# Start addresses of the matmul operands moved to multiples of 64 bytes, and 64 key tiles done in products of 256 columns

## The chip, the cores and the metric

The kernel runs on one core of one Trainium2 chip. The metric is the device time of one execution in microseconds (us); lower is better. Engines are named as the profile names them: PE is the matrix engine (PEld its weight loads), DVE the vector engine, ACT the scalar engine, POOL the GpSimd engine, SP the engine whose queue issues most transfers.

## What is computed

One decoder block on 256 tokens of width 1024, in float32. A mixer (convolution and dilated attention, gated, with one output projection) is added to x; then a retrieval layer is added:

```
def peer(xn, w_q, sub_keys, u_tab, v_tab):
    q = (xc @ w_q).reshape(TOKEN_CHUNK, PEER_HEADS, 2, half)
    s = einsum('thpd,hpnd->thpn', q, sub_keys)
    top_s, top_i = top_k(s, 16); ... best_s, best_c = top_k(cand, 16)
    e = i1 * PEER_N_KEYS + i2                      # expert of 16384
    gate = softmax(best_s)
    h = einsum('thkd,td->thk', u_tab[e], xc)
    act = gelu(h) * gate
    return einsum('thk,thkd->td', act, v_tab[e])
```

The kernel does not gather experts. It multiplies the tokens with all 16384 rows of u_tab and all 16384 rows of v_tab, and masks by a gate matrix.

## The kernel before

All data pass through 128 partitions. Weights come as 332 tiles of 128 partitions by 1024 float32 values (512 KB): 76 front tiles (projections of the mixer and the queries), 128 tiles of u_tab (the key tiles), 128 tiles of v_tab (the value tiles). Each tile goes through a ring of four slots in three buffers. SP loads it into `raw`; ACT rounds it to `hi` (`split_hi`, L335); POOL or DVE writes the remainder `raw - hi` to `lo` (`split_lo`, L354). Tokens and activations are split in the same way, so a float32 product is the sum of three products in the type float32r: hi with hi, hi with lo, lo with hi. `by_dve` (L337) says who makes which remainder: POOL alone in the first 64 key tiles, POOL and DVE by turns in the last 64 and in the last 64 value tiles, DVE alone in the first 64 value tiles.

The stages, in order of time:

- the front, 0 to some 255 us. `product` (L1236) does a slice of 128 weights by 256 tokens in three matmuls of 256 columns, with one weight load for each matmul. A tile is eight slices, 24 matmuls. The tokens are read from `nrm` (a view of `norm_space`) or from `rounded` (a view of `rounded_space`). L1266 and L1273 do the same in two loops for the first three tiles, L1343 with tokens as the weights for six tiles.
- the first 64 key tiles, some 259 to 435 us: `u_tile` (L1483), the same 24 matmuls, banks 4 and 5 by turns. ACT reads the bank through Gelu into `act` (`gelu`, L642). Beside it DVE selects the experts.
- the last 64 key tiles, some 435 to 632 us: `wide_tile` (L1489). Since `nrm` holds hi and lo of a slice side by side, the two products of `hi` are one matmul of 512 columns (L1499), and `lo` with the hi tokens one of 256 (L1501): 16 matmuls for a tile. The bank then holds two halves that must be added. ACT copies one half to `half_sum` (`copy_cross`, L666), DVE adds the other (`add_halves`, L1167), ACT applies Gelu to the sum (`gelu_sum`, L671). Beside it, every four tiles, DVE makes one-hot matrices for 16 tokens and PE multiplies them to gates (`gates`, L1513, 32 short matmuls of 64 columns in float16), and DVE multiplies the gates into `act` (L1154).
- the value tiles, some 632 to 1004 us: `v_tile` (L1554). The weights of PE are here activations (`act_hi`, `act_lo`, a second view of `norm_space`, filled by ACT at L677 and DVE at L1161), and `hi` or `lo` of the value tile is what streams, in 12 matmuls of 512 columns a tile (L1564; the last two tiles at L1590). In the first 64 tiles the gates of the other half of `act` are made as before.

Each engine's program is written out by hand with semaphores; nothing is reordered by a planner. PE waits for the remainder of its tile (`wait_lo`), and before it reuses bank 4 or 5 for what reads that bank.

Buffers lie one behind the other in the order of the code. The constant `SHIFT = 8` puts `nrm` 32 bytes behind the start of `norm_space`, and `rounded` 128 bytes behind that of `rounded_space`:

```
norm_space = sb("norm_space", [P, KB * 2 * T + SHIFT], F32R)
nrm = norm_space[:, SHIFT:].rearrange("p (k a t) -> p k a t", a=2, t=T)
picked_acts = norm_space[:, 0:RING * 2 * T].rearrange(...)
```

Of the kernel before, what the change touches and what calls it, by code (L numbers as in the profile page):

```python
# [15 lines left out]
P = 128  # L16
D = 1024
# [29 lines left out]
SHIFT = 8  # L47
# [117 lines left out]
def hybrid_block(nc, x_t, front, cols, rel_bias, onehot, sub_keys, u_tiles, v_tiles, out):  # L165
    bias_row = nc.dram_tensor("bias_row", (HEADS, BW), F32, kind="Internal").ap()
    toeplitz = nc.dram_tensor("toeplitz", (HEADS, P * BW), F32, kind="Internal").ap()
    with ExitStack() as ctx:
        def sb(name, shape, dt=F32, stack=ctx):
            return stack.enter_context(nc.sbuf_tensor(name, shape, dt))  # L170

        def sem(name):
            return ctx.enter_context(nc.semaphore(name))
# [7 lines left out]
        picked_acts = norm_space[:, 0:RING * 2 * T].rearrange("p (k a t) -> p k a t", a=2, t=T)  # L181
# [45 lines left out]
        half_sum = sb("half_sum", [P, 2, T])  # L227
        ohB = sb("ohB", [P, 2, TOK // PAIR, 2, HALF, PAIR], F16)
        raw = sb("raw", [P, RING, D])
        hi = sb("hi", [P, RING, D], F32R)  # L230
        lo = sb("lo", [P, RING, D], F32R)
# [61 lines left out]
        crossed, added, gelu_done = sem("crossed"), sem("added"), sem("gelu_done")  # L293
# [35 lines left out]
        def split_hi(act_e, base, it, j):  # L329

            s = slot_of(base, j)
            wait_raw(act_e, base, it, j)
            if not (isinstance(it, int) and base + 4 * it + j < RING):
                wait(act_e, pe_step, step_of(base - 4, it, j))
            act_e.copy(hi[:, s, :], raw[:, s, :]).then_inc(hi_ready, 1)  # L335
# [129 lines left out]
        def _(a):  # L465
# [196 lines left out]
            def copy_cross(it, j):  # L662

                a.wait_ge(pe_step, it * 4 + (S_U + HALF + j + 1))
                a.wait_ge(gelu_done, it * 4 + (HALF + j - 1))
                a.copy(half_sum[:, j % 2, :], bank[4 + j % 2][:, T:2 * T]).then_inc(crossed, 1)  # L666

            def gelu_sum(base, it, j):

                a.wait_ge(added, it * 4 + (base + j + 1))  # L670
                a.activation(act[:, it * 4 + (HALF + base + j), :], half_sum[:, (base + j) % 2, :], ACT.Gelu)\  # L671
                 .then_inc(gelu_done, 1)

# [5 lines left out]
            def key_round(it, first=False, last=False):  # L679
                for j in range(RING):  # L680
                    if last and j == RING - 1:
                        a.wait_ge(gated, GROUPS_N)
                        a.wait_ge(blocks_free, 1)
                        for first_act in range(AHEAD):
                            a_split(first_act, 0, 0)
                    copy_cross(it, j)
                    if not (first and j == 0):
                        gelu_sum(-1, it, j)
                    split_hi(a, U0 + HALF + LEAD, it, j)

            key_round(0, first=True)
            with a.Fori(1, HALF // RING - 1) as it:
                key_round(it)
            key_round(HALF // RING - 1, last=True)
            gelu_sum(HALF - 1, 0, 0)
# [22 lines left out]
        def _(dve):  # L718
# [445 lines left out]
            def add_halves(it, j):  # L1164

                dve.wait_ge(crossed, it * 4 + (j + 1))
                dve.tensor_tensor(half_sum[:, j % 2, :], bank[4 + j % 2][:, 0:T], half_sum[:, j % 2, :], ALU.add)\  # L1167
                   .then_inc(added, 1)

            def gate_body(half, it, first=False, last=False):  # L1170

                base = U0 + HALF if half == 0 else V0
                for j in range(RING):
# [16 lines left out]
                    if half == 0:  # L1190
                        if last and j == RING - 1:
                            for first_act in range(AHEAD):
                                low_part(first_act, 0, 0)
                        add_halves(it, j)
# [27 lines left out]
        def _(pe):  # L1222
# [260 lines left out]
            def u_tile(base_i, it, j):  # L1483

                wait(pe, gelu_done, it * 4 + (base_i + j - 1))
                ins = product(bank[4 + j % 2][:, 0:T], j, [(k, k) for k in range(KB)], nrm_hi, nrm_lo, U0 + base_i, it, j)
                ins.then_inc(pe_step, 1)

            def wide_tile(it, j, last=False):  # L1489

                b = bank[4 + j % 2]
                if isinstance(it, int) and it == 0 and j < 2:
                    pe.wait_ge(gelu_done, HALF + j - 1)
                else:
                    pe.wait_ge(added, it * 4 + (j - 1))
                wait_lo(pe, U0 + HALF, it, j)
                for k in range(KB):
                    unit = slice(k * P, (k + 1) * P)
                    pe.matmul(b[:, :], hi[:, j, unit], nrm[:, k, :, :].rearrange("p a t -> p (a t)"),  # L1499
                              start=k == 0, stop=False, skip_group_check=True)  # L1500
                    ins = pe.matmul(b[:, 0:T], lo[:, j, unit], nrm_hi[:, k, :],  # L1501
                                    start=False, stop=k == KB - 1, skip_group_check=True)
                    if last and k == RING - 1:
                        ins.then_inc(blocks_free, 1)
                ins.then_inc(pe_step, 1)
# [37 lines left out]
            def u_and_gates(it, last=False):  # L1543
                for j in range(RING):
                    for g in groups_ahead(it, j):
                        gates(0, it, g)
                    wide_tile(it, j, last and j == RING - 1)
# [117 lines left out]
```

## Time and profile before

| | |
|---|---|
| median of 2 runs | 1012.49 us (1012.19 to 1012.79) |
| profiled execution, its own time | 1012.39 us |
| span of the profile, first to last instruction | 1010.6 us |
| busy, share of the span | PE 100%, PEld 89%, DVE 79%, ACT 52%, POOL 46% |
| mean granted TensorE clock | 1.000 of full speed |

The span is the time between the first and the last instruction of the trace; the 1.8 us between it and the run's time lie outside the instructions. In the timeline, a row's first number is the start in us, the second how long it and what is merged with it took, and the count at the end how many instructions are merged. Matmuls overlap: one of 256 columns shows 0.28 us, but the next starts 0.11 us later. So the price of a matmul in a stream is read from start to start, not from its duration.

### The profile page before, as it was taken

The page shows a single profiled execution, that of the slowest core. Times are in us where ns is not written, and L with a number is a line of the kernel's source. Part 1 is how long each engine was busy: PE and PEld are TensorE (multiplying, and loading weights), DVE is VectorE, ACT ScalarE, POOL GpSimd, SP SyncE. Part 2 cuts the span into 40 slices and gives each one's busy share as a digit, 9 for nine tenths or more (in the row PEclk, how much of TensorE's full clock was granted, in tenths as well). Part 3 has the DMA queues.
Part 4 walks back from the last instruction along what each step waited for, and adds up shares of the span by engine and source line. Part 5 has one row for each costly group of instructions (what it writes and reads, how often), then busy time and mean ns, then how long its engine had stood idle before and what let it go on. Part 6 is the DMA issues. An engine that isn't in the chain of part 4 may idle for free.

```text
span 1010.6 us, 21094 instructions
## 1 busy us (share of the span) xinstructions
PE 1006.0 (100%) x7310; PEld 898.7 (89%) x7310; DVE 794.4 (79%) x1368; ACT 526.2 (52%) x853; POOL 460.8 (46%) x198
## 2 busy tenths in 40 slices
PE   9999999999999999999999999999999999999998
PEld 9999999999999999988888888788888888888886
DVE  6999785867999993288888888988888867676764
ACT  6654877644545445545555555544444444444443
POOL 4654456756699999943444433100000004444442
DMA  6684446655455566545554455555555555655562
GB/s 240 225 290 157 132 147 201 200 183 167 149 187 193 181 205 201 192 153 170 175 172 166 166 166 168 192 184 176 174 166 166 170 183 173 201 176 197 177 198 83
DMA packets 52618, 181.93 MB, mean 180 GB/s; under 512 B 5943, under 2 KB 9155, under 8 KB 52452
## 3 DMA queue, kind: packets, MB, share of 16 engines
q1 hardware_dynamic: 52292, 181.16, 54.2%
q8 instruction: 24, 0.39, 0.2%
q10 hardware_dynamic: 288, 0.27, 0.1%
q14 instruction: 14, 0.11, 0.0%
HBM read 180.33 MB, written 3.43 MB: 182 GB/s over the span
## 4 chain that ended last, share of the span: by engine, by line
PE 97%; ACT 1%; DVE 1%; issue 0%; POOL 0%; DVEq 0%; ACTq 0%; POOLq 0%
PE bank L1564 35%; PE bank L1242 33%; PE bank L1499 12%; PE bank L1501 6%; PE bank L1513 3%; PE bank L1343 2%; PE bank L1257 1%; PE bank L1475 1%; PE bank L1590 1%; PE bank L1266 1%; ACT hi L335 1%; PE bank L1359 1%; PE bank L1382 0%; DVE lo L354 0%; PE bank L1370 0%
## 5 line engine op out<-in xcount | busy, mean ns | idle before, releaser
L354 POOL TENSOR_TENSOR lo<-raw,hi 128x1024 fp32r<-128x1024 f32 x184 | 457.9, 2503 | 535.3 <-ACT hi L335 535.0
L335 ACT CAST hi<-raw 128x1024 fp32r<-128x1024 f32 x332 | 347.3, 1047 | 224.0 <-PE bank L1564 193.5
L1564 PE MATMUL bank<-hi,norm_space 128*128 128x512 f32 x1008 | 280.3, 397 | 0.0
L1242 PE MATMUL bank<-norm_space,hi 128*128 128x256 f32 x1600 | 276.4, 278 | 0.2 <-POOL lo L354 0.2
L1242 PEld LDWEIGHTS bank<-norm_space,hi 128*128 128x128 f32 x1600 | 241.6, 188 | 1.8 <-issue 1.2
L1564 PEld LDWEIGHTS bank<-hi,norm_space 128*128 128x128 f32 x1008 | 187.9, 188 | 44.6
L354 DVE TENSOR_TENSOR lo<-raw,hi 128x1024 fp32r<-128x1024 f32 x148 | 189.4, 1280 | 44.3 <-ACT hi L335 41.7
L1242 PE MATMUL bank<-norm_space,lo 128*128 128x256 f32 x800 | 221.6, 277 | 0.0
L1499 PE MATMUL bank<-norm_space,hi 128*128 128x512 f32 x512 | 182.8, 400 | 0.0
L1564 PE MATMUL bank<-lo,norm_space 128*128 128x512 f32 x504 | 158.3, 395 | 0.0
L1161 DVE TENSOR_TENSOR norm_space<-act,norm_space 128x256 fp32r<-128x256 f32 x128 | 111.2, 871 | 50.3 <-ACT norm_space L677 50.3
L1242 PEld LDWEIGHTS bank<-norm_space,lo 128*128 128x128 f32 x800 | 150.3, 188 | 0.0
L1501 PE MATMUL bank<-norm_space,lo 128*128 128x256 f32 x512 | 143.8, 281 | 0.0
L1499 PEld LDWEIGHTS bank<-norm_space,hi 128*128 128x128 f32 x512 | 96.3, 188 | 22.8
L1564 PEld LDWEIGHTS bank<-lo,norm_space 128*128 128x128 f32 x504 | 94.6, 188 | 22.8
L1501 PEld LDWEIGHTS bank<-norm_space,lo 128*128 128x128 f32 x512 | 96.2, 188 | 0.0
L1242 PE MATMUL bank<-rounded_space,hi 128*128 128x256 f32 x496 | 87.0, 280 | 0.0
L1242 PEld LDWEIGHTS bank<-rounded_space,hi 128*128 128x128 f32 x496 | 75.3, 188 | 0.9 <-issue 0.6
L666 ACT COPY half_sum<-bank 128x256 f32<-128x256 f32 x64 | 23.9, 374 | 92.1 <-PE bank L1501 92.1
L1242 PE MATMUL bank<-rounded_space,lo 128*128 128x256 f32 x248 | 69.1, 278 | 0.0
L645 ACT ACTIVATE act<-bank 128x256 f32 x64 | 24.6, 384 | 83.7 <-PE bank L1242 83.7
L1136 DVE TENSOR_TENSOR eqB<-iota_nk,keys 128x512 f16<-128x512 f16 x64 | 60.5, 945 | 0.1
(190 smaller groups left out, 955.4 us busy)
## 6 DMA issues: line engine op xcount, KB each, us to landing
raw<-u_tiles SPq DMA_DIRECT2D x128, 512.0 KB, 3.3
raw<-v_tiles SPq DMA_DIRECT2D x128, 512.0 KB, 3.3
raw<-front SPq DMA_DIRECT2D x76, 512.0 KB, 4.0
toeplitz<-bias_row SPq DMA_DIRECT2D x6, 384.0 KB, 7.4
bias<-toeplitz SPq DMA_DIRECT2D x12, 128.0 KB, 4.0
resid<-x_t SPq DMA_DIRECT2D x2, 512.0 KB, 4.6
qk<-sub_keys SPq DMA_DIRECT2D x1, 1024.0 KB, 7.7
y<-act SPq DMA_DIRECT2D x3, 256.0 KB, 2.0
```

The costliest lines, as they stand in the source:

```text
L335: act_e.copy(hi[:, s, :], raw[:, s, :]).then_inc(hi_ready, 1)
L354: eng.tensor_tensor(lo[:, s, :], raw[:, s, :], hi[:, s, :].bitcast(F32), ALU.subtract)\
L645: a.activation(act[:, it * 4 + (base_i + j), :], bank[4 + j % 2][:, 0:T], ACT.Gelu).then_inc(gelu_done, 1)
L666: a.copy(half_sum[:, j % 2, :], bank[4 + j % 2][:, T:2 * T]).then_inc(crossed, 1)
L1136: dve.tensor_tensor(eqB[:, :, :, :], every_pair(iota_nk[:, half * HALF:(half + 1) * HALF, :], HALF), at(keys[:, 1, t], HALF), ALU.is_equal ...
L1161: dve.tensor_tensor(act_lo[:, s, :], act[:, it * 4 + (base_i + j), :], act_hi[:, s, :].bitcast(F32), ALU.subtract).then_inc(a_lo, 1)
L1242: ins = pe.matmul(dst, w_[:, s, u * P:(u + 1) * P], x_[:, k, :], start=first and i == 0 and p_ == 0, stop=last and i == n - 1 and p_ == 2)
L1343: ins = pe.matmul(b[:, c * T:(c + 1) * T], x_[:, k, c * P:(c + 1) * P], w_[:, n % RING, 2 * m * P:2 * (m + 1) * P], start=k == 0 and c == ...
L1499: pe.matmul(b[:, :], hi[:, j, unit], nrm[:, k, :, :].rearrange("p a t -> p (a t)"), start=k == 0, stop=False, skip_group_check=True)
L1501: ins = pe.matmul(b[:, 0:T], lo[:, j, unit], nrm_hi[:, k, :], start=False, stop=k == KB - 1, skip_group_check=True)
L1513: ins = pe.matmul(bank[6 + g][:, q * HALF:(q + 1) * HALF], ohA[:, g, q // PAIR, :, q % PAIR], ohB[:, g, q // PAIR, i, :, q % PAIR], start= ...
L1564: ins = pe.matmul(bank[2 * c + half][:, :], a_[:, j, c * P:(c + 1) * P], v_[:, j, half * 512:(half + 1) * 512], start=False, stop=False, s ...
```

## The change

Three things, all in the layout and in the last 64 key tiles.

First, `SHIFT` becomes 0, `half_sum` is gone, and `raw`, `hi` and `lo` are cut out of larger buffers, with 448 bytes behind `raw` and 256 behind `hi`. Second, the slots of `hi` and `lo` are 4160 bytes apart and no longer 4096; those of `raw` stay 4096 apart. The start addresses in a partition, as the program is laid out:

| operand | before: byte, modulo 64 | after: byte, modulo 64 |
|---|---|---|
| `nrm` (tokens) | 16544, 32 | 16512, 0 |
| `act_hi` (activations as weights) | 16512, 0 | 16512, 0 |
| `rounded` (tokens) | 141472, 32 | 141312, 0 |
| `raw`, slot 0 | 178400, 32 | 176320, 0 |
| `hi`, slot 0 | 194784, 32 | 193152, 0 |
| `lo`, slot 0 | 211168, 32 | 210048, 0 |
| `sq` (squares, float32) | 44608, 0 | 44576, 32 |

A block of 128 columns is 512 bytes. Modulo 512, every slot of `hi` and `lo` began 64 bytes behind `nrm` before; after the change the four slots begin 0, 64, 128 and 192 bytes behind it.

Third, `wide_tile`, `copy_cross`, `add_halves` and `gelu_sum` go; the last 64 key tiles are done by `u_tile` and `gelu` like the first 64. The last of them is cut in two so that `blocks_free` is still signalled behind its fourth slice.

```diff
-SHIFT = 8
+SLOT_STEP, RAW_PAD, PART_PAD = 16, 112, 64
+SHIFT = 0
+ACT_SHIFT = 0
...
-        half_sum = sb("half_sum", [P, 2, T])
         ohB = sb("ohB", [P, 2, TOK // PAIR, 2, HALF, PAIR], F16)
-        raw = sb("raw", [P, RING, D])
-        hi = sb("hi", [P, RING, D], F32R)
-        lo = sb("lo", [P, RING, D], F32R)
+        raw_space = sb("raw_space", [P, RING * D + RAW_PAD])
+        raw = raw_space[:, 0:RING * D].rearrange("p (r d) -> p r d", r=RING)
+        hi_space = sb("hi_space", [P, RING * (D + SLOT_STEP) + PART_PAD], F32R)
+        lo_space = sb("lo_space", [P, RING * (D + SLOT_STEP)], F32R)
+        hi, lo = [x[:, 0:RING * (D + SLOT_STEP)].rearrange("p (r d) -> p r d", r=RING)[:, :, 0:D]
+                  for x in (hi_space, lo_space)]
...
-            def copy_cross(it, j):
-
-                a.wait_ge(pe_step, it * 4 + (S_U + HALF + j + 1))
-                a.wait_ge(gelu_done, it * 4 + (HALF + j - 1))
-                a.copy(half_sum[:, j % 2, :], bank[4 + j % 2][:, T:2 * T]).then_inc(crossed, 1)
...
+                    split_hi(a, U0 + HALF + LEAD, it, j)
                     if last and j == RING - 1:
                         a.wait_ge(gated, GROUPS_N)
                         a.wait_ge(blocks_free, 1)
                         for first_act in range(AHEAD):
                             a_split(first_act, 0, 0)
-                    copy_cross(it, j)
-                    if not (first and j == 0):
-                        gelu_sum(-1, it, j)
-                    split_hi(a, U0 + HALF + LEAD, it, j)
...
+                    gelu(HALF, it, j)
...
-            def add_halves(it, j):
-
-                dve.wait_ge(crossed, it * 4 + (j + 1))
-                dve.tensor_tensor(half_sum[:, j % 2, :], bank[4 + j % 2][:, 0:T], half_sum[:, j % 2, :], ALU.add)\
-                   .then_inc(added, 1)
...
-            def u_tile(base_i, it, j):
+            def u_tile(base_i, it, j, last=False):
 
                 wait(pe, gelu_done, it * 4 + (base_i + j - 1))
-                ins = product(bank[4 + j % 2][:, 0:T], j, [(k, k) for k in range(KB)], nrm_hi, nrm_lo, U0 + base_i, it, j)
-                ins.then_inc(pe_step, 1)
-
-            def wide_tile(it, j, last=False):
...
-                for k in range(KB):
-                    unit = slice(k * P, (k + 1) * P)
-                    pe.matmul(b[:, :], hi[:, j, unit], nrm[:, k, :, :].rearrange("p a t -> p (a t)"),
-                              start=k == 0, stop=False, skip_group_check=True)
-                    ins = pe.matmul(b[:, 0:T], lo[:, j, unit], nrm_hi[:, k, :],
-                                    start=False, stop=k == KB - 1, skip_group_check=True)
-                    if last and k == RING - 1:
-                        ins.then_inc(blocks_free, 1)
+                b, units = bank[4 + j % 2][:, 0:T], [(k, k) for k in range(KB)]
+                if last:
+                    product(b, j, units[:RING], nrm_hi, nrm_lo, U0 + base_i, it, j, last=False).then_inc(blocks_free, 1)
+                    ins = product(b, j, units[RING:], nrm_hi, nrm_lo, U0 + base_i, it, j, first=False)
                 else:
-                    pe.wait_ge(added, it * 4 + (j - 1))
-                wait_lo(pe, U0 + HALF, it, j)
+                    ins = product(b, j, units, nrm_hi, nrm_lo, U0 + base_i, it, j)
                 ins.then_inc(pe_step, 1)
...
-                    wide_tile(it, j, last and j == RING - 1)
+                    u_tile(HALF, it, j, last and j == RING - 1)
```

On PE, the loop over the last key tiles reads like this before (from the gates of one group to the second slice of the next tile; L1513 is `gates`, L1499 and L1501 are `wide_tile`):

```order
L1513 MATMUL bank<-ohB,ohA 128x64 x16
L1499 MATMUL bank<-norm_space,hi 128x512
L1501 MATMUL bank<-norm_space,lo 128x256
L1499 MATMUL bank<-norm_space,hi 128x512
L1501 MATMUL bank<-norm_space,lo 128x256
L1499 MATMUL bank<-norm_space,hi 128x512
```

And like this after it (L1480 is `gates`, L1222 is `product`):

```order
L1480 MATMUL bank<-ohB,ohA 128x64 x16
L1222 MATMUL bank<-norm_space,hi_space 128x256 x2
L1222 MATMUL bank<-norm_space,lo_space 128x256
L1222 MATMUL bank<-norm_space,hi_space 128x256 x2
L1222 MATMUL bank<-norm_space,lo_space 128x256
```

The pair of 512 and 256 columns of a slice has become three matmuls of 256 columns; the gates stand where they stood.

On ACT, a tile of that stage before, from the middle of the first round (L335 is `split_hi`, L666 `copy_cross`, L671 `gelu_sum`):

```order
L666 COPY half_sum<-bank 128x256
L671 ACTIVATE act<-half_sum 128x256
L335 CAST hi<-raw 128x1024
L666 COPY half_sum<-bank 128x256
L671 ACTIVATE act<-half_sum 128x256
L335 CAST hi<-raw 128x1024
```

And in the loop after it (L339 is `split_hi`, L649 `gelu`):

```order
L339 CAST hi_space<-raw_space 128x1024
L648 REGISTER_ALU
L649 ISA
L649 ACTIVATE act<-bank 128x256
L339 CAST hi_space<-raw_space 128x1024
```

The copy is gone, the Gelu reads the bank itself, and the rounding of the tile three ahead now stands before the Gelu of its own tile, where it stood behind the copy.

## Rows read from the trace of the kernel before

**Rows 1.** The page: the chain that ended last, share of the span.

```profile
PE 97%; ACT 1%; DVE 1%; issue 0%; POOL 0%; DVEq 0%; ACTq 0%; POOLq 0%
```

**Rows 2.** Windows: us, then busy us (instructions) of PE, PEld, DVE, ACT, POOL; PEclk, DMA share, GB/s.

```profile
35.00:75.00 40.00, 39.85 (x340) 39.39 (x340) 39.40 (x88) 24.06 (x44) 26.94 (x11) 1.00 0.83 282
208.00:255.00 47.00, 47.00 (x402) 46.89 (x401) 31.94 (x46) 19.78 (x27) 30.84 (x13) 1.00 0.53 174
255.00:440.00 185.00, 185.00 (x1628) 184.28 (x1628) 148.19 (x420) 95.37 (x140) 164.86 (x64) 1.00 0.56 184
440.00:640.00 200.00, 200.00 (x1554) 173.61 (x1553) 166.23 (x231) 109.42 (x199) 77.32 (x32) 1.00 0.51 169
640.00:832.00 192.00, 192.00 (x1236) 154.80 (x1235) 161.51 (x247) 84.83 (x125) 0.00 (x0) 1.00 0.53 175
```

**Rows 3.** Timeline of PE, first key tiles: start, us, instruction, count merged.

```profile
300.06 0.39 PE L1242 MATMUL bank<-norm_space,hi 128*128 128x256 f32 x2
...
311.62 0.39 PE L1242 MATMUL bank<-norm_space,hi 128*128 128x256 f32 x2
```

**Rows 4.** Timeline of PE, front, query projection.

```profile
240.01 0.40 PE L1242 MATMUL bank<-rounded_space,hi 128*128 128x256 f32 x2
...
247.43 0.40 PE L1242 MATMUL bank<-rounded_space,hi 128*128 128x256 f32 x2
```

**Rows 5.** Timeline of PE, last key tiles.

```profile
500.10 0.40 PE L1499 MATMUL bank<-norm_space,hi 128*128 128x512 f32 x1
...
507.52 0.40 PE L1499 MATMUL bank<-norm_space,hi 128*128 128x512 f32 x1
```

**Rows 6.** Timeline of PE, value tiles.

```profile
949.96 0.62 PE L1564 MATMUL bank<-lo,norm_space 128*128 128x512 f32 x2
950.42 1.56 PE L1564 MATMUL bank<-hi,norm_space 128*128 128x512 f32 x6
951.83 0.63 PE L1564 MATMUL bank<-lo,norm_space 128*128 128x512 f32 x2
952.29 0.63 PE L1564 MATMUL bank<-hi,norm_space 128*128 128x512 f32 x2
952.76 0.62 PE L1564 MATMUL bank<-lo,norm_space 128*128 128x512 f32 x2
```

**Rows 7.** The page, groups: count, busy us, mean ns, idle before.

```profile
L354 POOL TENSOR_TENSOR lo<-raw,hi 128x1024 fp32r<-128x1024 f32 x184 | 457.9, 2503 | 535.3 <-ACT hi L335 535.0
L335 ACT CAST hi<-raw 128x1024 fp32r<-128x1024 f32 x332 | 347.3, 1047 | 224.0 <-PE bank L1564 193.5
L1242 PE MATMUL bank<-norm_space,hi 128*128 128x256 f32 x1600 | 276.4, 278 | 0.2 <-POOL lo L354 0.2
L1499 PE MATMUL bank<-norm_space,hi 128*128 128x512 f32 x512 | 182.8, 400 | 0.0
L666 ACT COPY half_sum<-bank 128x256 f32<-128x256 f32 x64 | 23.9, 374 | 92.1 <-PE bank L1501 92.1
L645 ACT ACTIVATE act<-bank 128x256 f32 x64 | 24.6, 384 | 83.7 <-PE bank L1242 83.7
```

**Rows 8.** Timeline of PE, float32 products of 128 columns between two others.

```profile
252.03 7.31 PE L1475 MATMUL bank<-qk,prob 128*128 128x128 f32 x64
259.16 0.47 PE L1242 MATMUL bank<-norm_space,hi 128*128 128x256 f32 x2
```

**Rows 9.** Timeline of PE, float32 products of 256 columns from `sq`.

```profile
209.91 0.59 PE L1455 MATMUL bank<-sq,ones 128*128 128x256 f32 x2
210.34 0.59 PE L1456 MATMUL bank<-sq,ones 128*128 128x256 f32 x2
```

**Rows 10.** Timeline of PE, gate products in the value tiles, two rounds.

```profile
644.12 1.14 PE L1513 MATMUL bank<-ohB,ohA 128*128 128x64 f16 x32
...
656.39 1.14 PE L1513 MATMUL bank<-ohB,ohA 128*128 128x64 f16 x32
```

**Rows 11.** Groups of DVE in the last key tiles: count, busy us, mean ns, idle before.

```profile
L1167 DVE TENSOR_TENSOR half_sum<-bank,half_sum 128x256 f32<-128x256 f32 x63 | 26.3, 417 | 20.5 <-ACT half_sum L666 20.5
```

More of the change, by code:

```diff
@@ L180, in hybrid_block @@
         nrm_hi, nrm_lo = nrm[:, :, 0, :], nrm[:, :, 1, :]
-        picked_acts = norm_space[:, 0:RING * 2 * T].rearrange("p (k a t) -> p k a t", a=2, t=T)
+        picked_acts = norm_space[:, ACT_SHIFT:ACT_SHIFT + RING * 2 * T].rearrange("p (k a t) -> p k a t", a=2, t=T)
         act_hi, act_lo = picked_acts[:, :, 0, :], picked_acts[:, :, 1, :]
@@ L292, in hybrid_block @@
         sc_ready = sem("sc_ready")
-        crossed, added, gelu_done = sem("crossed"), sem("added"), sem("gelu_done")
+        gelu_done = sem("gelu_done")
         top_done, gexp, gate_ready, pick_T, pick_ready = [sem(s) for s in (
@@ L661, in _ @@
             a.wait_ge(pick_ready, 2)
-            def copy_cross(it, j):
-                a.wait_ge(pe_step, it * 4 + (S_U + HALF + j + 1))
-                a.wait_ge(gelu_done, it * 4 + (HALF + j - 1))
-                a.copy(half_sum[:, j % 2, :], bank[4 + j % 2][:, T:2 * T]).then_inc(crossed, 1)
[L668 to L672, printed above, removed]
             def a_split(base_i, it, j):
@@ L677, in a_split, with key_round @@
                 a.copy(act_hi[:, (base_i + j) % RING, :], act[:, it * 4 + (base_i + j), :]).then_inc(a_hi, 1)
-            def key_round(it, first=False, last=False):
+            def key_round(it, last=False):
                 for j in range(RING):
+                    split_hi(a, U0 + HALF + LEAD, it, j)
                     if last and j == RING - 1:
@@ L685, in key_round @@
                             a_split(first_act, 0, 0)
-                    copy_cross(it, j)
-                    if not (first and j == 0):
-                        gelu_sum(-1, it, j)
-                    split_hi(a, U0 + HALF + LEAD, it, j)
-            key_round(0, first=True)
-            with a.Fori(1, HALF // RING - 1) as it:
+                    gelu(HALF, it, j)
+            with a.Fori(0, HALF // RING - 1) as it:
                 key_round(it)
             key_round(HALF // RING - 1, last=True)
-            gelu_sum(HALF - 1, 0, 0)
             a.wait_ge(pe_step, S_V)
@@ L1189, in gate_body @@
                         one_hots(1, 0, j - 1)
[L1190 to L1194, printed above, removed]
+                    if half == 0 and last and j == RING - 1:
+                        for first_act in range(AHEAD):
+                            low_part(first_act, 0, 0)
                     if by_dve(base + LEAD, j):
@@ L1481, in _ @@
                     freed(pe, job)
-            def u_tile(base_i, it, j):
+            def u_tile(base_i, it, j, last=False):
                 wait(pe, gelu_done, it * 4 + (base_i + j - 1))
-                ins = product(bank[4 + j % 2][:, 0:T], j, [(k, k) for k in range(KB)], nrm_hi, nrm_lo, U0 + base_i, it, j)
-                ins.then_inc(pe_step, 1)
-            def wide_tile(it, j, last=False):
-                b = bank[4 + j % 2]
-                if isinstance(it, int) and it == 0 and j < 2:
-                    pe.wait_ge(gelu_done, HALF + j - 1)
-                else:
-                    pe.wait_ge(added, it * 4 + (j - 1))
-                wait_lo(pe, U0 + HALF, it, j)
-                for k in range(KB):
-                    unit = slice(k * P, (k + 1) * P)
-                    pe.matmul(b[:, :], hi[:, j, unit], nrm[:, k, :, :].rearrange("p a t -> p (a t)"),
-                              start=k == 0, stop=False, skip_group_check=True)
-                    ins = pe.matmul(b[:, 0:T], lo[:, j, unit], nrm_hi[:, k, :],
-                                    start=False, stop=k == KB - 1, skip_group_check=True)
-                    if last and k == RING - 1:
-                        ins.then_inc(blocks_free, 1)
+                b, units = bank[4 + j % 2][:, 0:T], [(k, k) for k in range(KB)]
+                if last:
+                    product(b, j, units[:RING], nrm_hi, nrm_lo, U0 + base_i, it, j, last=False).then_inc(blocks_free, 1)
+                    ins = product(b, j, units[RING:], nrm_hi, nrm_lo, U0 + base_i, it, j, first=False)
+                else:
+                    ins = product(b, j, units, nrm_hi, nrm_lo, U0 + base_i, it, j)
                 ins.then_inc(pe_step, 1)
```

## Prediction

> **What bounds the kernel now.** I read the page's chain first, then the windows by stage, then the timeline of PE in each stage. [...] Durations don't help here: a matmul of 256 columns shows 278 ns and one of 512 shows 400 [rows 7], but they overlap. The starts say this:
>
> - first key tiles: from 300.06 to 311.62 us stand 34 slices of three matmuls, 0.340 us a slice, 113.3 ns a matmul [rows 3];
> - query projection, the same three matmuls: 240.01 to 247.43 is 21 slices, 0.3533 us, 117.8 ns a matmul [rows 4];
> - last key tiles: 500.10 to 507.52 is 21 pairs of 512 and 256 columns, 0.3533 us a pair [rows 5];
> - value tiles: 949.96 to 952.76 is twelve matmuls of 512 columns, 2.80 us, 233.3 ns each [rows 6].
>
> [...] Every token and weight that streams now starts in the middle of a piece of 64 bytes, so 256 columns touch 17 pieces and 512 touch 33. [...]
>
> **The change part by part.** The sum is against the profiled execution's own time, 1012.39 us (span 1010.6 and 1.8 around it); the median of the runs is 1012.49, the same.
>
> *Three matmuls of 256 columns, aligned.* The trace has no aligned float32r stream long enough to price. [...] From above: the dear 117.8 of [rows 4]. [...] A slice becomes 0.3345 us.
>
> - First key tiles: 64 tiles of 8 slices, 512 slices, 0.340 to 0.3345: 2.8 us less. (Bounds: 6.8 more if they fall to the dear rate.)
> - Front: 1608 matmuls of the `product` line outside the 1536 of the key tiles, 72 in the first three tiles and 144 with tokens as weights are 1824, 608 slices. By the starts in the timeline some 890 of them (297 slices) run at the dear rate; the windows show it, 402 instructions in 47 us are 117 ns each and 340 in 40 us are 118, against 1628 in 185 us, 114, in the first key tiles [rows 2]. 608 x 0.0055 is 3.3, and 297 x 0.0133 is 4.0: 7.3 us less. (Bounds: 4.1 more, if the 311 cheap slices turn dear, to 7.3 less.)
>
> *Last key tiles.* 512 pairs at 0.3533 become 512 slices at 0.3345: 9.6 us less. With no help from the alignment a slice costs 0.340 or 0.3533 [rows 3, 4], 6.8 less or nothing. The gates between them don't change. ACT loses a copy of 374 ns a tile [rows 7], DVE an addition of 417 [rows 11]: 24 and 27 us of work that no one waited for, worth nothing. The bank is now free after the Gelu, and the Gelu stands behind a rounding on ACT. That is 1047 + 384 ns [rows 7] in a tile of 2.7 us, the chain that the first key tiles already have, where PE never waits.
>
> *Value tiles.* 1512 matmuls and the last 24, of 512 columns. One unit less makes 226.7 ns, 1536 x 6.67 is 10.2 us less. The nearest aligned row is the pair of square sums: `sq` starts at a multiple of 64, and two float32 products of 256 columns start 209.91 to 210.34 us, 215 ns each [rows 9]. [...] The upper bound is one unit more than now, 240 ns, 10.2 more. [...]
>
> [...]
>
> *What could uncover another engine.* POOL makes all remainders in the first key tiles: 164.86 us for 64 tiles in the window, 2.58 us each [rows 2], and PE will take 24 x 111.5, 2.68. It still fits with 0.1 us. DVE in the first value tiles is busy 161.5 of 192 us, 10.3 us of a round of 12.27 (644.12 to 656.39, [rows 10]); four tiles fewer by 0.08 make the round 11.95. It fits too. The new slot distance may change how fast these engines run; a POOL that took 2.8 us would cost 64 x 0.12, 8 us.
>
> Sum: 2.8 + 7.3 + 9.6 + 10.2 = 29.9 us, 1012.4 - 29.9 = 982.5 us.
>
> **The rivals.**
>
> *All overhead of the value tiles goes* (collisions too). At 215 ns, 28.2 us instead of 10.2: 964.5 us. For it: [rows 9] and the fact that weights and stream in this stage now stand at different places within 64 bytes, which ends. Against: the row is at half rate. [...]
>
> *The alignment does nothing.* Rates stay two for slices and 233.3 ns for the value tiles; only the last key tiles change, to something between 0.340 and 0.3533. Each gate group pauses PE, so both rates would come: half of 6.8 us, 1009 us (1005.6 to 1012.4). [...] The four matmuls that spread the key norms have aligned operands and show no visibly shorter steps, though these are in the first starts after a pause, which are always irregular.
>
> *Collisions get worse; slower.* [...] Before, a slot stood 64 bytes behind the tokens in every case; now the four slots stand at 0, 64, 128 and 192. If the 64 bytes were what allowed the 0.340 rate, the first key tiles lose it (512 x 0.0133, 6.8 us), the cheap slices of the front too (311 x 0.0133, 4.1), the last key tiles gain nothing, and the value tiles take one more unit (1536 x 6.67 ns, 10.2): 21.1 us more, 1033.5 us. It decides from the point where the extra collision is more than the piece saved, that is above 0.3533 a pair and 2.80 us a value tile.
>
> **How the numbers follow.** A measurement of this kernel can tell about 2% from no change, 20 us. The forecast, with a spread of 973 to 994 by the bounds of the slices, gets 0.43; all overhead gone 0.18; no effect of the alignment 0.24; slower by collisions 0.15. Faster by over 2% means below 992.2: the first rival and nearly all of the forecast, 0.58. Slower by over 2% (above 1032.7) is two thirds of the last case, 0.1. Between lies 0.32. The range for 8 in 10 reaches from the first rival to the upper end of the second, 963 to 1014, and leaves out most of the slower case.
>
> **What would show it.** In the timeline of PE: starts in the first key tiles 0.3345 us a slice (34 slices in 11.37 us), the same in the last key tiles and the whole front, with one rate where there are two; twelve value matmuls in 2.72 us. PE's idle time must stay at nothing, POOL and DVE must keep their durations. The forecast is wrong if the value tiles keep 2.80 (the second rival), if they show 2.58 (the first), or if the step depends on the slot, which would be collisions by distance. If PE waits for a remainder in the first key tiles, POOL is the bound.

## The result

The changed kernel takes 1022.38 us, the median of two runs (1022.34 to 1022.43), against 1012.49 before: the ratio is 1.0097, with a 95% interval of 1.0073 to 1.0121. It is slower by 1%. The forecast was 982.5 and the range ended at 1014.

The chain of the page is PE as before, and PE is busy for the whole span of 1020.5 us. This line answers to [rows 1]:

```profile
PE 98%; ACT 1%; DVE 0%; POOL 0%; issue 0%; ACTq 0%; POOLq 0%
```

So no wait was added; PE does its matmuls at a longer step. The windows of the changed kernel answer to [rows 2] (us, then busy us and instructions of PE, PEld, DVE, ACT, POOL, then the granted clock):

```profile
208.00:255.00 47.00, 47.00 (x396) 46.90 (x396) 31.18 (x41) 20.36 (x27) 28.71 (x13) 1.00 0.51 172
255.00:440.00 185.00, 185.00 (x1567) 185.00 (x1566) 132.99 (x422) 92.15 (x135) 161.98 (x64) 1.00 0.54 178
440.00:640.00 200.00, 200.00 (x2059) 199.26 (x2058) 147.19 (x163) 86.85 (x130) 84.35 (x34) 1.00 0.51 170
640.00:832.00 192.00, 192.00 (x1290) 156.99 (x1289) 163.72 (x249) 86.24 (x130) 2.88 (x2) 1.00 0.52 172
```

In the 185 us from 255 PE starts 1567 matmuls where it started 1628, at the same granted clock of 1.00. The groups that make the remainders and the roundings have kept their durations (POOL 2503 ns before and 2521 now, ACT 1047 in both; compare [rows 7]):

```profile
L358 POOL TENSOR_TENSOR lo_space<-raw_space,hi_space 128x1024 fp32r<-128x1024 f32 x184 | 461.8, 2521 | 541.5 <-ACT hi_space L339 541.3
L339 ACT CAST hi_space<-raw_space 128x1024 fp32r<-128x1024 f32 x332 | 347.1, 1047 | 227.0 <-PE bank L1531 192.8
L1222 PE MATMUL bank<-norm_space,hi_space 128*128 128x256 f32 x2624 | 470.3, 282 | 0.2 <-POOL lo_space L358 0.2
```

The timeline of PE in the first key tiles, read as in [rows 3], is where it shows. These are the first matmuls of five tiles in a row, slots 0, 1, 2, 3 and 0 again (start in us, duration, instruction):

```profile
274.54 0.40 PE L1222 MATMUL bank<-norm_space,hi_space 128*128 128x256 f32 x2
...
277.41 0.40 PE L1222 MATMUL bank<-norm_space,hi_space 128*128 128x256 f32 x2
...
280.24 0.40 PE L1222 MATMUL bank<-norm_space,hi_space 128*128 128x256 f32 x2
...
283.09 0.40 PE L1222 MATMUL bank<-norm_space,hi_space 128*128 128x256 f32 x2
...
285.91 0.40 PE L1222 MATMUL bank<-norm_space,hi_space 128*128 128x256 f32 x2
```

A tile of 24 matmuls took 2.72 us in every slot before, in 60 of the 62 first key tiles that the next tile follows at once. Now slot 0 takes 2.87, slot 1 2.83, slot 2 2.85 and slot 3 2.82. The step depends on the slot, which the prediction named as the sign of collisions by distance.

That it is the distance and not the slot shows already in the front. There the tokens come from `rounded`, and by the table of addresses the four slots of `hi` start 128, 192, 256 and 320 bytes behind it instead of 0, 64, 128 and 192. These are the first matmuls of five tiles in a row of the query projection, slots 2, 3, 0, 1 and 2 again:

```profile
238.89 0.40 PE L1222 MATMUL bank<-rounded_space,hi_space 128*128 128x256 f32 x2
...
241.76 0.40 PE L1222 MATMUL bank<-rounded_space,hi_space 128*128 128x256 f32 x2
...
244.59 0.40 PE L1222 MATMUL bank<-rounded_space,hi_space 128*128 128x256 f32 x2
...
247.44 0.40 PE L1222 MATMUL bank<-rounded_space,hi_space 128*128 128x256 f32 x2
...
250.26 0.40 PE L1222 MATMUL bank<-rounded_space,hi_space 128*128 128x256 f32 x2
```

The 2.87 us are now slot 2's, and 2.83, 2.85 and 2.82 those of slots 3, 0 and 1. Slot 2 at 256 costs what slot 0 at 0 cost in the key tiles (2.87), slot 0 at 128 what slot 2 cost at 128 (2.85).

The value tiles went the other way (to be set against [rows 6]): four tiles, 48 matmuls, from 905.43 to 916.52 us, 11.09 us where it was 11.20.

```profile
905.43 1.56 PE L1531 MATMUL bank<-hi_space,norm_space 128*128 128x512 f32 x6
...
916.52 1.56 PE L1531 MATMUL bank<-hi_space,norm_space 128*128 128x512 f32 x6
```

By stage, from the first start of one to the first start of the next in both traces (the last key tiles begin with their first gate products):

| stage | before, us | after, us | difference |
|---|---|---|---|
| front | 259.2 | 263.1 | +3.9 |
| first key tiles | 174.9 | 182.7 | +7.8 |
| last key tiles | 198.2 | 199.5 | +1.3 |
| value tiles but the last two | 369.5 | 366.4 | -3.1 |

The rest of the span is the same, so this is the 9.9 us by which the spans differ (1010.6 and 1020.5).

### The profile page after: what moved, and what is told of

Same layout as the page of the kernel before. It is cut to its first block, busy times and chain, and to the rows that moved or that the text cites. A ratio compares the mean times of both kernels' runs of the same rounds, so it can differ in the third digit from the quotient of the medians.

```text
span 1020.5 us, 21854 instructions
## 1 busy us (share of the span) xinstructions
PE 1015.9 (100%) x7822; PEld 936.6 (92%) x7822; DVE 765.5 (75%) x1304; ACT 506.8 (50%) x789; POOL 464.7 (46%) x198
## 4 chain that ended last, share of the span: by engine, by line
PE 98%; ACT 1%; DVE 0%; POOL 0%; issue 0%; ACTq 0%; POOLq 0%
PE bank L1222 53%; PE bank L1531 34%; PE bank L1480 3%; PE bank L1323 2%; PE bank L1237 1%; PE bank L1455 1%; PE bank L1246 1%; PE bank L1557 1%; PE bank L1339 1%; PE bank L1362 0%; ACT hi_space L339 0%; PE bank L1350 0%; DVE lo_space L358 0%; PE bank L1253 0%; PE bank L1300 0%; PE bank L1290 0%
## 5 line engine op out<-in xcount | busy, mean ns | idle before, releaser
L358 POOL TENSOR_TENSOR lo_space<-raw_space,hi_space 128x1024 fp32r<-128x1024 f32 x184 | 461.8, 2521 | 541.5 <-ACT hi_space L339 541.3
L1222 PE MATMUL bank<-norm_space,hi_space 128*128 128x256 f32 x2624 | 470.3, 282 | 0.2 <-POOL lo_space L358 0.2
L339 ACT CAST hi_space<-raw_space 128x1024 fp32r<-128x1024 f32 x332 | 347.1, 1047 | 227.0 <-PE bank L1531 192.8
L1222 PEld LDWEIGHTS bank<-norm_space,hi_space 128*128 128x128 f32 x2624 | 403.3, 189 | 1.8 <-issue 1.2
L1222 PE MATMUL bank<-norm_space,lo_space 128*128 128x256 f32 x1312 | 368.7, 281 | 0.0
L1531 PE MATMUL bank<-hi_space,norm_space 128*128 128x512 f32 x1008 | 278.0, 395 | 0.0
L1222 PEld LDWEIGHTS bank<-norm_space,lo_space 128*128 128x128 f32 x1312 | 247.8, 189 | 0.0
L1531 PEld LDWEIGHTS bank<-hi_space,norm_space 128*128 128x128 f32 x1008 | 188.0, 188 | 42.1
L358 DVE TENSOR_TENSOR lo_space<-raw_space,hi_space 128x1024 fp32r<-128x1024 f32 x148 | 186.7, 1262 | 31.6 <-ACT hi_space L339 30.1
L1531 PE MATMUL bank<-lo_space,norm_space 128*128 128x512 f32 x504 | 157.4, 393 | 0.0
L649 ACT ACTIVATE act<-bank 128x256 f32 (+1 forms) x128 | 49.2, 384 | 203.3 <-PE bank L1222 203.2
L1222 PE MATMUL bank<-rounded_space,hi_space 128*128 128x256 f32 x496 | 88.9, 282 | 0.0
L1222 PEld LDWEIGHTS bank<-rounded_space,hi_space 128*128 128x128 f32 x496 | 76.4, 189 | 0.8 <-issue 0.6
L1222 PE MATMUL bank<-rounded_space,lo_space 128*128 128x256 f32 x248 | 69.7, 281 | 0.0
L1222 PEld LDWEIGHTS bank<-rounded_space,lo_space 128*128 128x128 f32 x248 | 46.8, 189 | 0.0
```

Source lines behind the costliest of these rows:

```text
L358: eng.tensor_tensor(lo[:, s, :], raw[:, s, :], hi[:, s, :].bitcast(F32), ALU.subtract)\
L649: a.activation(act[:, it * 4 + (base_i + j), :], bank[4 + j % 2][:, 0:T], ACT.Gelu).then_inc(gelu_done, 1)
L1222: ins = pe.matmul(dst, w_[:, s, u * P:(u + 1) * P], x_[:, k, :], start=first and i == 0 and p_ == 0, stop=last and i == n - 1 and p_ == 2)
L1531: ins = pe.matmul(bank[2 * c + half][:, :], a_[:, j, c * P:(c + 1) * P], v_[:, j, half * 512:(half + 1) * 512], start=False, stop=False, s ...
```

## The experiments

Steps below are means in ns from start to start, by slot where slots differ. In the key tiles the rate that a tile holds is taken within it, without its first steps, where tiles are counted by rate; other means go from the first start of a tile to that of a later one. In the value tiles they are taken from the first start of a tile to that of the next, because the single steps go in threes there (231, 231, 238 in the kernel before, 233.3 in the mean) and a part of a tile gives a wrong mean. "Distance" is the number of bytes, modulo 512, between the start of the weights and the start of what streams: `hi` and `lo` behind the tokens in the key tiles, `hi` and `lo` behind the activations in the value tiles. In the changed kernel it is 0, 64, 128, 192 by slot in both. It is counted from tokens to `hi` in one case and from activations to `hi` in the other, so from the stream to the weights in the key tiles and from the weights to the stream in the value tiles.

Two theories were set against each other first. Theory D: the step is set by this distance, not by where the start lies within 64 bytes. Theory A: the start within 64 bytes matters, one way or the other, the recorded forecast being one form of it.

### The third part alone

```diff
-SLOT_STEP, RAW_PAD, PART_PAD = 16, 112, 64
-SHIFT = 0
+SHIFT = 8
...
+        half_sum = sb("half_sum", [P, 2, T])
...
+        raw = sb("raw", [P, RING, D])
+        hi = sb("hi", [P, RING, D], F32R)
+        lo = sb("lo", [P, RING, D], F32R)
```

This and the diffs below are against the changed kernel, where nothing else is said.

> Edit: the kernel before with only the third part of the change (last 64 key tiles in 24 matmuls of 256 columns, no copy and no addition); every start address as before. Theory D (distance): what sets the pace is the distance in bytes between where a weight block starts and where the streamed block starts; it is 64 for every slot here, as in the first key tiles, so after a pause PE takes 113.3 or 117.8 ns a matmul and keeps it until the next pause. The gates pause it every four tiles, so the last key tiles take between 0.340 and 0.3533 us a slice: 1005.6 to 1012.4 us, value tiles unchanged at 233.3 ns. Theory N (the narrow form itself is what made the changed kernel slower): the last key tiles take more than 0.3533 us a slice and the time is above 1012.4, near 1022.

Measured: 1006.28 us (1006.01 to 1006.51), ratio 0.9942 (0.992 to 0.9965). The last key tiles stand at 113.3 ns a matmul in 62 of the 64 tiles, and at 117.8 in two. The timeline, to be set against [rows 5]: 17 slices from 500.13 to 505.91, 0.340 us a slice instead of 0.3533.

```profile
500.13 0.39 PE L1219 MATMUL bank<-norm_space,hi 128*128 128x256 f32 x2
...
505.91 0.39 PE L1219 MATMUL bank<-norm_space,hi 128*128 128x256 f32 x2
```

The kernel before took 1012.26 us beside it, so the narrow form saves 6.0 us; by the trace the last key tiles are 6.1 us shorter and the other stages unchanged within 0.2. The new layout costs the other way, 1022.4 - 1006.3 = 16.1 us.

### Aligned, with one distance of 64

```diff
-SLOT_STEP, RAW_PAD, PART_PAD = 16, 112, 64
+SLOT_STEP, RAW_PAD, PART_PAD = 0, 0, 0
+ROUNDED_SHIFT = 32
...
-        rounded = rounded_space[:, 4 * SHIFT:].rearrange("p (b t) -> p b t", t=T)
+        rounded = rounded_space[:, ROUNDED_SHIFT:].rearrange("p (b t) -> p b t", t=T)
```

> Edit: the changed kernel with the slots of hi and lo 4096 bytes apart again and placed so that every slot starts 64 bytes behind nrm and behind rounded (modulo 512), as before, but everything at multiples of 64. It differs from e1 in the alignment (and by the activations). Theory D (distance, not alignment): the first key tiles run at 113.3 ns again, and the value tiles, where the streamed tile now starts 64 bytes behind the activations for all slots, run at the 228.5 ns that slot 1 showed in the changed kernel: 1012.4 - 7.7 = 1004.7 us, or some 998 if the last key tiles are at 113.3 too. Theory A (alignment is what harms: starts at multiples of 64 never hold 113.3): first and last key tiles at 117.8 ns, the time near 1012 even with cheap value tiles. My own reading on record (a matmul pays one piece of 64 bytes less when aligned): 111.5 ns and 226.7.

Measured: 1000.32 us (999.96 to 1000.68), ratio 0.9883 (0.9854 to 0.9911). 113.3 ns in the first key tiles in all slots, and value tiles at 228.9. Of the last key tiles 60 held 113.3 as well, four 117.8. The timeline of PE, 32 slices in 10.88 us:

```profile
300.09 0.39 PE L1223 MATMUL bank<-norm_space,hi_space 128*128 128x256 f32 x2
...
310.97 0.39 PE L1223 MATMUL bank<-norm_space,hi_space 128*128 128x256 f32 x2
```

That is 0.340 us, the very price of [rows 3], with everything at a multiple of 64. Whether the operands start at 0 or at 32 modulo 64 neither costs nor gains here (113.3 ns in both): theory A falls in both its forms, and with it the recorded 111.5.

### The changed kernel, all moved by 32 bytes

```diff
-SHIFT = 0
-ACT_SHIFT = 0
+SHIFT = 8
+ACT_SHIFT = 8
```

> Edit: the changed kernel with nrm, act, rounded, raw, hi and lo all moved by 32 bytes, so that nothing starts at a multiple of 64, while all distances between them (0, 64, 128, 192 by slot) stay. Theory D: the same time as the changed kernel, 1022.4 within 1, and by slot 119.9, 117.8, 118.5, 117.8 ns in the key tiles. Theory A: the first key tiles return to 113.3 ns in at least the slots at distance 64, and the time falls below 1015.

Measured: 1022.37 us (1022.37 to 1022.38), against 1022.38 for the changed kernel. By slot 119.6, 117.9, 118.7, 117.7 ns in the first key tiles and 228.3, 230.3, 232.9, 232.9 in the last value tiles (from the first matmul of a tile to the first of the next), the changed kernel's own numbers within 0.1. Without the first six matmuls of a tile the key tiles of both have 119.9, 117.9, 118.5 and 117.7. Whether all starts are 0 or 32 modulo 64 makes no difference.

### Only the activations moved

Against the kernel before:

```diff
-        picked_acts = norm_space[:, 0:RING * 2 * T].rearrange("p (k a t) -> p k a t", a=2, t=T)
+        picked_acts = norm_space[:, SHIFT:SHIFT + RING * 2 * T].rearrange("p (k a t) -> p k a t", a=2, t=T)
```

> Edit: the kernel before with only the activations of the value tiles moved 32 bytes up, so that in the value tiles the streamed tile starts 64 bytes behind the weights (modulo 512) where it started 96 behind. Theory D: value tiles at 228.5 ns a matmul instead of 233.3 (1536 x 4.8 = 7.4 us), 1005 us, all else as before. Theory A or any theory of one start address alone: the streamed operand has not moved, so value tiles stay at 233.3 and the time at 1012.4; if the start of the weights alone counts, they could get dearer.

Measured: 1005.7 us (1005.48 to 1007.0), ratio 0.9939 (0.9916 to 0.9961). The value tiles went from 233.3 to 228.9 ns though the streamed tile had not moved. Their weights had, and with them the distance, from 96 to 64. Four tiles, 48 matmuls, take 10.99 us instead of 11.20:

```profile
902.19 1.54 PE L1564 MATMUL bank<-hi,norm_space 128*128 128x512 f32 x6
...
913.18 1.54 PE L1564 MATMUL bank<-hi,norm_space 128*128 128x512 f32 x6
```

Since e3 shows that 0 or 32 for all starts is the same, what counted here is the distance and not the place of the weights by itself (1022.37 us against 1022.38 with all moved, 1005.7 against 1012.26 with the weights alone).

### Without the stagger, and other distances

The open question was whether a distance has a price of its own or whether the change of distance from tile to tile costs. The first of these is the changed kernel with the stagger alone taken back; the others are e2 with `hi` and `lo` moved, their diffs against e2.

```diff
-SLOT_STEP, RAW_PAD, PART_PAD = 16, 112, 64
+SLOT_STEP, RAW_PAD, PART_PAD = 0, 112, 0
```

> Edit: the changed kernel with only the slots of hi and lo 4096 bytes apart again, so that every slot is where slot 0 was (distance 0 to nrm and to the activations, 128 to rounded). Theory D1 (each distance has its own price): all key tiles at the price of slot 0, 119.9 ns, the value tiles at 228.2; first key tiles 1536 x (119.9 - 118.5) = 2 us slower than in the changed kernel, last key tiles the same, value tiles 1536 x (230.6 - 228.2) = 3.7 us faster: some 1022 us. Theory D2 (the price comes from the distance changing at each tile, which breaks a phase that would otherwise hold): key tiles at 113.3 or 117.8 ns, the time between 1000 and 1012.

```diff
-SLOT_STEP, RAW_PAD, PART_PAD = 0, 0, 0
+SLOT_STEP, RAW_PAD, PART_PAD = 0, 160, 0
```

> Edit: as e2, but every slot of hi and lo starts 192 bytes behind nrm, rounded and the activations (modulo 512), as slot 3 of the changed kernel did. Theory D1: key tiles 117.8 ns and never 113.3, value tiles 233.3: slower than before or equal, some 1012 to 1016. Theory D2: key tiles hold 113.3 as with 64, value tiles by their own price, 1000 to 1006.

With `RAW_PAD` 120 and 136 the distance is 32 and 96:

> Edit: as e2 with a distance of 32 bytes between weights and stream everywhere; hi and lo at 32 modulo 64, tokens and activations at 0. No kernel has had it. Theory D1 with prices that rise and fall with distance: between the key prices of 0 (119.9) and 64 (113.3 possible), value tiles near 228.5, some 1000 to 1018. If distances count only in steps of 64, it equals 0 or 64.

> Edit: as e2 with a distance of 96 bytes everywhere. In the value tiles this is what the kernel before had: theory D says 233.3 ns there. In the key tiles nothing has had it; if 113.3 is possible the time is 1006, as e1, if only 117.8 it is 1018.

Measured: 1023.16 us (1022.78 to 1023.53) for distance 0, 1022.12 (1021.94 to 1022.3) for 192, 1025.34 (1024.8 to 1025.88) for 32 and 1025.31 (1024.82 to 1025.79) for 96. All are slower than the kernel before, which took 1012.19 beside them. With one distance for all slots the first key tiles of e5 run at 120.0 ns (60 of 62), 32 slices in 11.52 us:

```profile
300.06 0.40 PE L1222 MATMUL bank<-norm_space,hi_space 128*128 128x256 f32 x2
...
311.58 0.40 PE L1222 MATMUL bank<-norm_space,hi_space 128*128 128x256 f32 x2
```

This is slot 0 of the changed kernel without its neighbours. So each distance has a price of its own: 120.0, 117.8, 118.3 and 118.7 ns in the key tiles at 0, 192, 32 and 96. The stagger gave the four slots four distances, three of them poor ones. It also spoilt the good one: slot 1 of the changed kernel is at distance 64, but ran at 117.8 ns in all of its 32 key tiles, where a kernel with 64 in every slot holds 113.3 (all 64 first key tiles of e2 behind their first matmuls). By these two steps that is 32 x 24 x 4.5 ns, an estimated 3.5 us. Why slot 1 keeps the dearer of its two rates behind a slot at distance 0 is not shown. The expectations for e6, e7 and e8 were too low: their value tiles came as expected for 192 and 96, at 233.3 ns, but I had undersized the front and, for 32 and 96, the key tiles. In e6 four of the first key tiles ran at 113.3, the other 60 and all 64 last ones at 117.8, so 192 has the two rates of 64 as well, but kept the dearer one in 124 of 128 tiles.

### The best of both, and how far it reaches

The table by then gave 64 as the one good distance for the key tiles and 0 for the value tiles. Tokens and activations are different views, so both can be had (against e2):

```diff
-ACT_SHIFT = 0
+ACT_SHIFT = 16
```

> Edit: e2 with only the activations moved 64 bytes up, so that weights and stream start at the same place (modulo 512) in the value tiles and 64 apart in the key tiles. Theory D1 (each distance its own price): key tiles 113.3 ns as in e2, value tiles 226.7 as in e5, 1536 x 2.2 ns = 3.4 us below e2: 997 us, faster than both kernels. Rival (the value price of e5 came from something else in its layout, such as hi and lo starting with the tokens): value tiles stay at 228.9, 1000.3 us.

Measured: 996.53 us (996.28 to 996.87), ratio 0.9839 (0.9822 to 0.9855). It is faster than both kernels, and hit its expectation of 997. The key tiles run at 113.3 and the value tiles at 226.7, twelve in 2.72 us (compare the 2.80 of [rows 6]):

```profile
949.50 1.52 PE L1532 MATMUL bank<-hi_space,norm_space 128*128 128x512 f32 x6
...
952.22 1.52 PE L1532 MATMUL bank<-hi_space,norm_space 128*128 128x512 f32 x6
```

Three more kernels looked at the period of the pattern and at how wide the good place is. With `RAW_PAD` 64 and `ACT_SHIFT` 80 the key distance is 320:

> Edit: as e9, but hi and lo start 320 bytes behind the tokens (64 and one half of 512 more), activations with them. Tells the period of the pattern. If it repeats every 256 bytes: key tiles at 113.3, 997 us. If it repeats every 512: key tiles at some 118 to 120 ns, 1012 to 1018 us.

For steps of 16 bytes the views of `hi` and `lo` begin 4 elements into their buffers:

```diff
-        hi, lo = [x[:, 0:RING * (D + SLOT_STEP)].rearrange("p (r d) -> p r d", r=RING)[:, :, 0:D]
+        hi, lo = [x[:, 4:4 + RING * (D + SLOT_STEP)].rearrange("p (r d) -> p r d", r=RING)[:, :, 0:D]
```

> Edit: as e9 with 48 bytes instead of 64 between tokens and weights of the key tiles. Theory D1 with a narrow best place at 64: key tiles at 115 to 118.5 ns, between 998 and 1015 us. If 48 is as good as or better than 64: 113.3 or less, 997 or below.

> Edit: as e9 with 80 bytes. Theory D1 with a narrow best place at 64: key tiles at 115 to 118.5 ns, between 998 and 1015 us. If 80 is as good as or better than 64: 113.3 or less, 997 or below.

Measured: 997.24 us (996.95 to 997.52) for 320, with the steps of e9, 113.3 and 226.7 ns. So 320 is as good as 64 in the key tiles, and by the front of the changed kernel 256 is as dear as 0, 2.87 us a tile: the pattern repeats after 256 bytes where two such distances were run. 1023.73 (1022.73 to 1024.73) for 48 and 1023.08 (1022.87 to 1023.29) for 80, with 117.8 ns in 58 of 62 first key tiles of e10 and 118.6 to 119.0 in 60 of 62 of e11. These two miss the expected 998 to 1015 as well. They are not clean: in the value tiles the distance is 0 as in e9, but weights and stream both start 16 bytes past a multiple of 32, and the step is not 226.7: it is 230.0 or 233.3 ns in e10 and 230.0 in e11, with 231.1 to 231.2 in some tiles of its first half. So a start off a multiple of 32 seems to have a price of its own. In the key tiles of e10 and e11 `hi` and `lo` start there too, so their 117.8 and 118.6 to 119.0 can't be put down to the distance alone. That the good place is narrow rests on 32 and 96 (118.3 and 118.7 ns, e7 and e8), where nothing starts off a multiple of 32.

All prices are in ns and from start to start. Key tiles: three matmuls of 256 columns, each with its weight load, mean of one. Value tiles: one of 512 columns. Each is read from the timeline of PE at a mean granted clock of 1.000, over the four tiles (96 or 48 matmuls) whose starts stand in the third and fifth column, in us (for the value tiles those of the rows of six merged matmuls, one a tile).

| distance, modulo 256 | key tiles | run: starts | value tiles | run: starts |
|---|---|---|---|---|
| 0 | 120.0 | e5: 301.14 to 312.66 | 226.7 | e5: 908.79 to 919.67; e9: 914.14 to 925.02 |
| 32 | 118.3 | e7: 308.52 to 319.88 | 233.3 | e7: 906.80 to 918.00 |
| 64 | 113.3 | e1: 302.93 to 313.81; e2: 302.81 to 313.69 | 228.9 | e2: 906.10 to 917.08; e4: 913.18 to 924.16 |
| 96 | 118.7 | e8: 308.68 to 320.07 | 233.3 | e8: 906.85 to 918.05; before: 905.62 to 916.83 |
| 128 | 118.7 | slot 2 of the changed kernel, one tile: 314.36 to 317.21 | 232.9 | slot 2 of the changed kernel, each of its 15 last value tiles that another follows: 2.795 us from first matmul to first |
| 192 | 117.8 | e6: 307.29 to 318.59 | 233.3 | e6: 915.14 to 926.34 |

Of the 62 first key tiles that the next tile follows at once, the step of the table is held by 60 at 0 (e5), 60 at 32 (e7) and 60 at 64 (e1 and e2, within 0.1); at 96 (e8) 58 stand between 118.5 and 118.8, and at 192 (e6) 58 at 117.7 or 117.8. The others at 0, 32 and 64 come first behind other matmuls, at 117.5 to 122.8. There are second rates: 117.8 at 64, as in [rows 4]; 113.3 at 192 in four tiles; 117.3 to 117.5 at 96, in two of the 62 and in 16 of the 31 last key tiles of slots 1 and 2 that the next tile follows at once. All 16 tiles of slot 2 of the changed kernel take 118.7 or 118.8.

The row of 128 is from a slot with neighbours at other distances. For the same products of 256 columns e5 has 128 in every slot in the part of the front that reads `rounded`: from the seventh matmul of a tile to its last, 17 tiles there ran at 118.4 to 118.9 and 14 at 119.8 to 120.0. So two rates for one distance are not peculiar to 64.

## Why the prediction was wrong

*What bounds the kernel*: PE, as the forecast took it. It was 97% of the chain before [rows 1] and busy all the time at a granted clock of 1.00 in every window from 208 to 832 us [rows 2], so that the time is the number of matmuls times their step. PE is 97% of the chain or more in every version but two, and the changed kernel added no wait of PE. In e1 and e9 (92% and 93%), where most tiles of the front run at the lower rate, DVE is 5% of the chain and PE waits for it once in the front, 0.9 and 0.8 us; so DVE may be why ten more tiles of the front at the lower rate did not shorten it in e1 (259.3 us against 259.2). The copy and the addition that went were worth nothing.

*The prices of the sum*: no run shows the 111.5 ns a matmul (0.3345 us a slice). It was my estimate, taken next to the 111.4 of [rows 8]; in every run the stream of 256 columns stood at 113.3 or above. The 6.67 ns less in the value tiles was an estimate too. It is half of what lies between the two slices, 0.3533 and 0.340 us, and in this unit the steps before are whole numbers: 113.3 is 17, three times 117.8 is 53, 233.3 is 35. Some of the new ones fit: 120.0 is 18 of them, 226.7 is 34, and three times 228.9 is 103. Others don't: three times 118.7 is 53.4, three times 230.0 is 103.5. One unit in each matmul I took for the piece of 64 bytes that a start in the middle of one adds, and that is the step that failed. The step of 113.3 is there with everything aligned (e2), and moving all starts by 32 bytes changes nothing (e3, 1022.37 against 1022.38). From a quantum in the prices I had concluded a cause, while all operands that stream in float32r stood at the same place within 64 bytes, so that the trace before could not tell the piece from a collision by distance. The price of 111.5 (down from 113.3) carried 2.8, 3.3 of 7.3 and 2.8 of the 9.6 us, and the same reading carried the 10.2 us of the value tiles. The remaining 4.0 of the front and 6.8 of the last key tiles rested on a second assumption, that the aligned kernel has one rate where there were two. It has both when it is aligned: in e2 31 of the 67 `product` tiles of the front run at 113.3 and the rest at 117.8. The price of 111.5 came in no stage.

*The nearest rows*: the float32 products of 128 columns at 111.4 and of 256 at 215 [rows 8, 9] are both at about half the rate of the float32r stream, which takes 113.3 for 256. They were too far from the case to lend it a price: no run shows the 215 ns of the first rival for 512 columns of float32r, nor the 111.5 for 256. No run held a mean step under 226.7 and 113.3.

*The narrow form*: its case without help from the alignment was 0 to 6.8 us; e1 measured 6.0, at the good end, since the good rate was taken up again after nearly every gate group. In the changed kernel it is covered: three slots had distances at which 0.340 us a slice came hardly ever (4 of 128 key tiles at 192 in e6) or never, slot 1 kept the dearer rate, and the last key tiles lost 1.3 us.

*Value tiles*: 10.2 us less was forecast, 3.1 came. The 226.7 ns of the forecast does exist, in e9, by distance 0 and not by the alignment. In the changed kernel slot 0 is near it (228.3), slot 1 at 230.3 and slots 2 and 3 at 232.9, against 233.3 before. That the stage got shorter at all is luck: the forecast had the sign by an alignment that neither costs nor gains (e2, e3).

*The rivals*: the one that ended slower had what the runs show, the distance between weights and stream, and said what would show it, a step that depends on the slot. Its sizes: first key tiles 6.8 us, measured 7.8; front 4.1, measured 3.9; last key tiles 0, measured 1.3; value tiles 10.2 more, measured 3.1 less. So 1033.5 was too much by the value tiles alone. It was given 0.15. The prediction had seen that the changed layout put three of four slots at other distances, and that the good rate had been read at no distance but 64; that spoke for a higher chance than 0.15.

As long as the distance stays, 32 bytes past a multiple of 64 is as good as 0 (e3, 1022.37 against 1022.38 us). Of 16 bytes past that can't be said: there e10 and e11 have value tiles at 230.0 to 233.3 ns where e9 has 226.7. Weights and stream are not independent in time in these runs: moving the weights alone by 32 bytes changed the step from 233.3 to 228.9 ns (e4). Where weight load and stream meet, no run shows. The lowest step of 512 columns in any run was 226.7.

What stays open: why these distances are the good ones, and why one distance can have two rates, such as 113.3 and 117.8 at 64, of which PE takes one after a pause and mostly keeps it: from one product tile to the next without a pause the rate changed between the two in none of 111 cases before, in none of 158 in e2, and in 4 of 159 in the changed kernel. In the front 33 of the 67 `product` tiles ran at the lower before and in e12, 31 in e2 and e4, 43 in e1 and e9, and no experiment steered that. In the changed kernel 5 did, and all five stood at distance 64 or 320.

## What to carry to other kernels

Where PE streams float32r without a pause, lay out the weights and the streamed operand by the distance between them, not by alignment, and keep that distance the same for every ring slot, since a good slot between poor ones lost its good rate here (117.8 ns for 113.3); in this kernel the offsets alone were worth 26 us of 1022 (1022.4 against 996.5). Tokens that stream against a tile and activations that are weights against it can want different distances (in e9 113.3 ns at 64 and 226.7 at 0), so give each view its own offset. When the prices in a trace are multiples of one unit, first ask whether any row varies the cause one has in mind; if none does, it is a guess. When steps go in cycles, take means over whole cycles.

## What was unexpected of the hardware

The step of a matmul depends on where its weights start relative to its stream: 113.3 to 120.0 ns for 256 columns, 226.7 to 233.3 for 512 columns, at a mean granted clock of 0.999 or 1.000 in all cases. It repeated after 256 bytes where that was run, with 256 columns: 2.87 us a tile at 0 and 256, 113.3 ns at 64 and 320. The order of the distances is not the same for the two: 0 is the best for the value tiles (226.7) and the dearest for the key tiles (120.0). A shift of both by 32 bytes cost nothing (1022.37 against 1022.38 us); a place 16 bytes off a multiple of 32 went with 3.3 to 6.7 ns more a matmul at the same distance in the value tiles (e11 and e10 against e9).
